# A decoder layer with 64 experts: the expert loops of all five engines are written out

## What is computed

```python
def moe_ffn(h, w_router, router_bias, w_gate_e, w_up_e, w_down_e, w_gate_s, w_up_s, w_down_s):
    scores = jax.nn.sigmoid(h @ w_router)                       # (512, 64)
    _, top_idx = lax.top_k(scores + router_bias, 8)
    top_s = jnp.take_along_axis(scores, top_idx, axis=-1)
    top_w = top_s / jnp.sum(top_s, axis=-1, keepdims=True) * 2.5
    gates = jnp.sum(jax.nn.one_hot(top_idx, 64) * top_w[..., None], axis=1)
    ...
        hg = jnp.einsum('td,edf->tef', xb, w_gate_e)            # w_gate_e: (64, 1024, 256)
        hu = jnp.einsum('td,edf->tef', xb, w_up_e)
        hmid = jax.nn.silu(hg) * hu * gb[..., None]
        return jnp.einsum('tef,efd->td', hmid, w_down_e)        # w_down_e: (64, 256, 1024)
    ...
    return routed + swiglu(h, w_gate_s, w_up_s, w_down_s)
```

## Time and profile before

| what | value |
|---|---|
| median of 3 runs | 1125.73 us (1122.69 to 1127.16) |
| span of the profiled execution | 1124.9 us |
| mean granted TensorE clock | 0.993 |
| busy: TensorE, VectorE, ScalarE, GpSimd | 97%, 78%, 66%, 28% of the span |
| instructions recorded | 19071 |
| DMA moved | 284.69 MB, of it 0.58 MB instructions |

### The profile page before, as it was taken

One profiled execution on the slowest core, in us unless ns is written; L12 is line 12 of the kernel. 1 busy time (PEld: TensorE's weight loads), 2 busy tenths in 40 slices (PEclk: granted clock), 3 DMA queues, 4 the chain that ended last, 5 costly groups with the idle time before them and its releaser, 6 DMA issues.

```text
span 1124.9 us, 19071 instructions
## 1 busy us (share of the span) xinstructions
PE 1088.4 (97%) x5809; PEld 895.3 (80%) x5809; DVE 881.4 (78%) x1405; ACT 738.8 (66%) x1304; POOL 317.3 (28%) x293
## 2 busy tenths in 40 slices
PE   8999999999999989999999999999999999999995
PEld 7789978777778877578888888888888788888784
DVE  6544475578766735579999999999999999999893
ACT  5434455443447411258888888888888888888783
POOL 1221011000000001126334343353354545433551
PEclk9999999999999999999999999999999999999998
DMA  7243221422422274559999999999999999999962
GB/s 245 76 114 113 75 76 39 150 75 73 135 75 95 86 298 186 207 195 400 383 390 379 387 383 384 380 377 378 385 369 369 375 385 373 376 380 388 344 190 36
DMA packets 69704, 284.69 MB, mean 253 GB/s; under 512 B 16611, under 2 KB 19179, under 8 KB 44700
## 3 DMA queue, kind: packets, MB, share of 16 engines
q1 hardware_dynamic: 51228, 250.50, 57.2%
q0 software_dynamic: 18432, 33.61, 12.5%
HBM read 279.79 MB, written 37.81 MB: 282 GB/s over the span
## 4 chain that ended last, share of the span: by engine, by line
DMA 45%; PE 36%; DVE 8%; issue 5%; POOL 3%; ACT 2%; POOLq 1%; SPq 0%; ACTq 0%; DVEq 0%
DMA out<-arena,idxs 43%; PE bank L1643 20%; PE bank L1791 3%; PE bank L1817 3%; PE bank L1587 2%; POOL turn L592 2%; PE bank L1831 2%; PE bank L1805 2%; DVE w_lo L1082 1%; ACT arena L782 1%; DMA arena<-in_w_out 1%; DMA arena<-hn_dram,idxg 1%; DVE gu_parts L1429 1%; PE bank L1699 1%; PE bank L1712 1%
## 5 line engine op out<-in xcount | busy, mean ns | idle before, releaser
L1817 PE MATMUL bank<-gu_parts,xT_parts 128*128 128x512 f32 x1280 | 339.1, 395 | 1.6 <-DVE gu_parts L1429 0.5
L1817 PEld LDWEIGHTS bank<-gu_parts,xT_parts 128*128 128x128 f32 x1280 | 235.3, 188 | 48.6 <-DVE gu_parts L1429 0.9
L1831 PE MATMUL bank<-w_lo 128*128 128x512 f32 x804 | 203.2, 402 | 1.0 <-DVE w_lo L1435 1.0
L592 POOL TENSOR_TENSOR turn<-minus_half 16x1 f32<-16x1 f32 x128 | 98.6, 770 | 351.5 <-DMA out<-arena,idxs 290.7
L1831 PEld LDWEIGHTS bank<-w_lo 128*128 128x128 f32 x804 | 147.5, 190 | 30.1 <-DVE w_lo L1435 1.1
L1643 PE MATMUL bank<-w_hi,hT_hi 128*128 128x512 f32 (+1 forms) x320 | 125.2, 391 | 4.3 <-DVE arena L1378 3.2
L602 POOL DMA_INDIRECT out<-arena,idxs x64 | 117.9, 1842 | 28.8 <-issue 26.3
L1643 PE MATMUL bank<-w_hi,hT_lo 128*128 128x512 f32 (+1 forms) x320 | 122.2, 382 | 0.0
L1643 PE MATMUL bank<-w_lo,hT_hi 128*128 128x512 f32 (+1 forms) x320 | 121.9, 381 | 0.0
L1429 DVE TENSOR_TENSOR gu_parts<-arena_x,gu_parts 128x1024 fp32r<-128x1024 f32 x96 | 116.7, 1215 | 1.0 <-ACT gu_parts L953 0.9
L1429 DVE TENSOR_TENSOR gu_parts<-arena,gu_parts 128x1024 fp32r<-128x1024 f32 x96 | 116.7, 1215 | 0.2 <-ACT gu_parts L953 0.2
(11 more groups left out here) (226 smaller groups left out, 1956.9 us busy)
## 6 DMA issues: line engine op xcount, KB each, us to landing
arena<-in_w_gate_e SPq DMA_DIRECT2D x32, 1024.0 KB, 8.7
arena<-in_w_up_e SPq DMA_DIRECT2D x32, 1024.0 KB, 12.0
arena<-in_w_down_e SPq DMA_DIRECT2D x32, 1024.0 KB, 7.1
arena_x<-in_w_gate_e SPq DMA_DIRECT2D x32, 1024.0 KB, 8.9
arena_x<-in_w_up_e SPq DMA_DIRECT2D x32, 1024.0 KB, 12.1
arena_x<-in_w_down_e SPq DMA_DIRECT2D x32, 1024.0 KB, 7.0
arena<-in_w_in SPq DMA_DIRECT2D x14, 1024.0 KB, 5.4
arena<-in_w_gate SPq DMA_DIRECT2D x8, 1024.0 KB, 5.6
```

Of the source, the lines that this page charges most:

```text
L592: nc.gpsimd.tensor_tensor(turn[:], minus_half[0:16, 0:1], minus_half[0:16, 0:1], ALU.add).then_inc(turns, 1)
L1817: last = nc.tensor.matmul(out_, a[:, PER * c + j, :], b[c][:, :, j, :], start=(c == 0 and j == 0 and i == 0), stop=(c == CHUNKS - 1 and j ...
L1831: last = nc.tensor.matmul(psY[h][0:rows, :], midT[n][a][:, j, 0:rows], w[b][:, j, h * 512:(h + 1) * 512], start=(j == 0 and k == 0), stop= ...
```

## The change

All five loops are replaced by Python loops, so that every step is written out, with numbers for the waits and addresses. Order and operations of the steps stay as they are; where a loop ended at a special case, the same case is now chosen by a condition.

```diff
-            regs = [sp.alloc_register(f"turn_value{i}") for i in range(2)]
-            with sp.Fori(1, E // 4) as m:
-                for n in range(4):
-                    k = 4 * m + n
-                    for reg, v in zip(regs, (CHUNKS * (k - 3), 2 * (k - 2))):
-                        sp.reg_mov(reg, v)
-                    read_gu, read_d = (bass.RuntimeValue.of_register_unchecked(r, min_val=1, max_val=2 * 16 * E) for r in regs)
-                    sp.wait_ge(gu_lo_ready, read_gu)
-                    load_w(n, 0, k)
-                    load_w(n, 1, k)
-                    sp.wait_ge(wd_ready, read_d)
-                    load_w(n, 2, k)
+            for k in range(4, E):
+                sp.wait_ge(gu_lo_ready, CHUNKS * (k - 3))
+                load_w(k % 4, 0, k)
+                load_w(k % 4, 1, k)
+                sp.wait_ge(wd_ready, 2 * (k - 2))
+                load_w(k % 4, 2, k)
...
-            for k in range(4):
-                pair(k, k)
-            with pool.Fori(1, (E - 5) // 4) as m:
-                for u in range(4):
-                    pair(4 * m + u, u)
-            for k in range((E - 5) // 4 * 4, E - 5):
+            for k in range(E - 5):
                 pair(k, k % 4)
...
-            for it in range(SH + 1, SH + 4):
-                step(it, it % 2, it % 4)
-            with act.Fori(SH // 4 + 1, ITEMS // 4 - 1) as m:
-                for u in range(4):
-                    step(4 * m + u, u % 2, u)
-            for it in range(ITEMS - 4, ITEMS):
+            for it in range(SH + 1, ITEMS):
                 step(it, it % 2, it % 4, more=it + 1 < ITEMS)
...
-            for k in range(4):
-                expert(k, k)
-            with dve.Fori(1, E // 4 - 2) as m:
-                for u in range(4):
-                    expert(4 * m + u, u)
-            for k in range(E - 8, E):
+            for k in range(E):
                 expert(k, k % 4, ix=k + 4 < E, oh=k + 5 < E, xt=k + 1 < E)
...
-            for it in range(3, SH + 4):
-                step(it, it % 4)
-            with pe.Fori(2, ITEMS // 4 - 1) as m:
-                for u in range(4):
-                    step(4 * m + u, u)
-            for it in range(ITEMS - 4, ITEMS):
-                step(it, it % 4, xt=it + 1 < ITEMS, ix=False)
+            for it in range(3, ITEMS):
+                step(it, it % 4, xt=it + 1 < ITEMS, ix=it < E)
```

## The result

| kernel | median | range | runs |
|---|---|---|---|
| before | 1126.26 us | 1122.14 to 1129.19 | 21 |
| loops written out | 1131.58 us | 1126.33 to 1135.99 | 21 |

The ratio is 1.005, with a 95% interval of 1.0037 to 1.0064: 5.3 us slower by the medians. The forecast was 1128, with 1116 to 1142 as its range. The profiled execution has a span of 1130.9 us against 1124.9, so the two traces can be compared for the same 6 us.

The account below looks back on a forecast made before the run. The prediction took TensorE, 97% busy, as the bound, with VectorE and DMA close to full. Terms 0 + 0 + 0 + 1 + 1 = +2 us on the profiled 1124.9 gave 1126.9, plus 0.8 to the median: 1128 us, range 1116 to 1142.

Parts of the forecast that it names:

- two terms of 1 us: The forecast's only nonzero terms: +1 us for GpSimd's chain of scatters and +1 us for added instruction fetch.
- TensorE, 0: Removing TensorE's loop control and register work beside matmuls gains 0, bounds -0.6 to +0.6 us.
- ScalarE and VectorE, 0: Removing these engines' register work gains 0, since operations are queued meanwhile; bounds 0 and -0.7 us.
- SyncE, 0: Removing SyncE's register moves lets weight loads go out slightly earlier, but no engine waits for them: gain 0.
- cover of 16 us: Weight loads land some 16 us before they are read, so issuing them earlier gains nothing.
- GpSimd, +1: GpSimd's chain from scatter landing to next issue gets slower written out: +1 us, bounds 0 and +3.1.
- 0.06 us: GpSimd's extra time per pair from a scatter's landing to the next issue: 0.92 us written out, 0.86 looped.
- Fetch, +1: Instruction packets fetched by DMA for the written-out experts: 20 large, 15 to 25 small; +1 us, bounds 0 and 22.
- the nearest row: The stretch from 500 to 600 us: 8 packets fetched, TensorE busy 98.88 of 100 us, so fetch was priced low.
- Late gathers are a lottery of the turns: GpSimd's small additions ahead of gathers (turns) are sometimes held about 5.8 us, by phase against VectorE, making five gathers late.
- the rival that counted on the turns: Faster by phase: without the five late gathers and low clock, 1114 to 1119, say 1117 us; chance 0.15, shared with edges.
- The rival by edges: Loop back edges stall for instruction fetch, so removing them is faster; said to add nothing to the faster rival's 0.15.

Follow-up runs that it names:

- e5: Only TensorE's loop written out, against the kernel before: 1126.27 us, ratio 1.0011.
- e10: Only ScalarE's and VectorE's loops written out, against the kernel before: 1129.26 us, ratio 1.0024.
- e9: Only SyncE's loop written out, against the kernel before: 1121.32 us, ratio 0.9960.
- e4: SyncE's loop written out plus 100 idle wait instructions per expert behind its down load, against the kernel before: 1196.08 us, ratio 1.0634.
- e12: SyncE's loop written out plus 100 idle wait instructions per expert between up and down loads; against the kernel before: 1151.76 us, ratio 1.0224.
- e6: Only GpSimd's loop written out, against the kernel before: 1125.05 us, ratio 1.0003.
- e2: All five loops written out, GpSimd's small addition ahead of each gather made a memset; against the kernel before: 1129.09 us, ratio 1.0033.
- e1: Only GpSimd's loop written out, its small addition ahead of each gather made a memset; against the kernel before: 1123.75 us, ratio 0.9993.
- e8: All loops written out but TensorE's, against the kernel before: 1131.23 us, ratio 1.0070.
- e7: All loops kept, 100 idle wait instructions per expert behind SyncE's down load inside its loop; against the kernel before: 1157.19 us, ratio 1.0295.

## Why the prediction was right, and where it was not

The range held the time, and the forecast, slightly slower, had the right sign and too small a size: 2 us where 5.3 were measured, which is just about the bound of 0.5%. The chain of reasons behind the number fared less well: of the two terms of 1 us one was worth nothing, and the other stands for a loss whose way was not found. That the sum came out on the right side is in part luck.

- *TensorE, 0*: right. 9.53 us an expert before and after, and e5 costs 0.1%, within its noise.
- *ScalarE and VectorE, 0*: right for the register work, which nobody waited for. But writing these two out alone costs 2.7 us (e10), whose cause is as open as that of the whole.
- *SyncE, 0*: not quite. Writing it out alone gave -0.4% (e9), and the cover of 16 us that I named is real for the weights, but e4 against e12 (same instructions and packets, waits at another place) shows that the place of a load in time can matter to others than those who read it: in e4 nothing on TensorE waits for a load, and the kernel is 6% slower.
- *GpSimd, +1*: the 0.06 us are there in every pair, and cost 0 (e6, from -1.5 to +2.1 us). The caution, that landings follow the weight loads and absorb it, fits this and was not tested by itself; zero would have been the better value.
- *Fetch, +1*: this is the term that was mis-sized, if the loss of the written-out streams is put down to it. By what is left when the other terms are 0 it is 5 us, and by e2 against e1 4 to 5. The number of packets was right (20 large and 15 to 25 small forecast, 22 and 18 found), and the bounds, 0 and 22, hold it. What probably misled was the nearest row: from 500 to 600 us TensorE waited for no gather (once for VectorE, 1.1 us) although 8 packets were fetched. From 500 to 600 us gathers land 4 to 17 us before TensorE's transposes read them (landings set beside the starts of the transposes, in the trace of before), and a disturbance there reaches nobody: a turn held for 5.49 us at 510.22, ahead of a gather, cost TensorE nothing. From 750 us on that stock is 1 to 6 us, but for those that are late, and a hold of the same length makes TensorE wait. I had read the absence of a wait as the absence of a cost. And packet time was the wrong measure: it gave the large packets the weight, and e5 and e8 show it the other way.
- *Late gathers are a lottery of the turns*: half right. The hold by VectorE's run is real, and all late gathers before and after stand behind one, but the turn is only one of the instructions that it can catch (e2), so the rival that counted on the turns had a wrong price for their absence: e1 took all of them away and gained 0.8 us by the ratio, not 7 to 9.
- *The rival by edges* (a stall at each back edge): no run shows any; e5, which removes TensorE's, is no faster.

## What to carry to other kernels

A loop whose engine has work queued ahead costs nothing, so writing it out can only lose by what it adds, here most likely instruction packets in a stage whose DMA engines are always busy. Which stream costs is to be measured one by one and not counted from instructions: TensorE's, the longest, cost 0.1% here, ScalarE's and VectorE's 0.2%, SyncE's and GpSimd's nothing. A row that shows no wait prices a disturbance only if the slack at that row is the slack at the place where the disturbance will be: read how early the transfer lands, not only whether somebody waits. And before an operation is blamed for a hold, ask which instruction stands behind it and would be held instead.

## What the runs showed of the hardware that was not expected

- An indirect DMA instruction on GpSimd is held like an addition while VectorE runs tensor_tensor operations on SBUF: 5.9 to 7.1 us in place of 1.04 to 1.9. In e1 the one at 827.35 ended at 833.24, and VectorE ran such operations from 827.69 to 832.32. A memset of 16 numbers was never held (0.6 us at most in 128, e1 and e2).
- Whether a loop body is fetched again is not a matter of its length alone. In the kernel before none was from 600 to 1000 us, though TensorE's body has about 477 recorded instructions; SyncE's body of 435 in e7 was, in every pass (49 packets of 8 KB in 400 us). TensorE's packets are of 16 KB (e5 adds only such), those of the other engines of 8 KB (e8 and e10 add only such).
- Sending the gate and up loads out some 6 us later, though no engine is seen waiting for them, came with 6% more time in e4 and with 3% in e7; e12, with e4's instructions and packets and the loads in place, is at 2%. e4's scatters took 9.0 us at least and 10.1 in the median.
- Small instruction packets came with more time than large ones: 30 us for 47 of 8 KB (e12 against e9, where SyncE also runs 6000 more instructions), 1.4 us for 22 of 16 KB (e5 against the kernel before beside it, within its noise).
